# Turning the block inverses with 64x64 products through two shared banks, in a new order on TensorE

## The reference, cut to what matters

```python
DN_CHUNK = 64          # 16 value heads, computed in 8 pairs
def chunk_gated_delta(q, k, v, g, beta, s0):
    ...
    a = jnp.where(strict, jnp.einsum('bhncd,bhnsd->bhncs', kb, kc) * decay, 0.0)
    eye = jnp.eye(DN_CHUNK, dtype=F32)
    t_inv = lax.linalg.triangular_solve(eye + a, jnp.broadcast_to(eye, a.shape),
                                        left_side=True, lower=True, unit_diagonal=True)
    u = jnp.einsum('bhncs,bhnse->bhnce', t_inv, vb)
    w = jnp.einsum('bhncs,bhnsd->bhncd', t_inv, kb * jnp.exp(gc)[..., None])
    ...
def bidir_delta(q, k, v, g, beta, s0_f, s0_b):      # d = 0 forwards, d = 1 backwards
    ...
def rwkv7_scan(r, w, k, v, kk, a, reverse):         # second block, both directions
    def step(s, inp):
        sa = jnp.einsum('bhvk,bhk->bhv', s, -kk_t)
        s = (s * w_t[:, :, None, :] + sa[..., None] * (kk_t * a_t)[:, :, None, :]
             + v_t[..., None] * k_t[:, :, None, :])
```

## Time and profile before

| | |
|---|---|
| times of the kernel before, 3 runs | 2149.61, 2157.09, 2621.62 us; median 2157.09 |
| span of the profiled execution | 2156.7 us |
| the profiled execution beside the median | 0.4 us under it |
| TensorE busy | 1964.5 us (91%) |
| VectorE, ScalarE, GpSimd busy | 1031.2, 594.5, 74.1 us |
| level products of the first block, L1049 and L1076 | 60.5 and 58.1 us busy |
| copies of the turned inverses, L1195 | 47.8 us busy in 80 |

### The profile page before, as it was taken

The page is one execution under the profiler, slowest core; times in us unless marked ns, Lnnn a source line. Parts: engine busy times, 40 slices in busy tenths (PEclk is TensorE's granted clock), DMA queues, the critical chain, the costliest instruction groups (busy, mean ns, idle before and its releaser), DMA issues. The chain is left out here.

```text
span 2156.7 us, 40120 instructions
## 1 busy us (share of the span) xinstructions
PE 1964.5 (91%) x16700; PEld 1441.6 (67%) x16700; DVE 1031.2 (48%) x2064; ACT 594.5 (28%) x1275; POOL 74.1 (3%) x50
## 2 busy tenths in 40 slices
PE   5789999999999999789888889988889899989998
PEld 2346666666666666534376677767776798878887
DVE  3346756675766757411125457775455543311101
ACT  1023434444343434300203223232332321000000
POOL 0000101000010101000000000000000000000000
PEclk8889999999999999989999989989999999999999
DMA  8801101010101010032131243221112112434443
GB/s 329 313 18 61 38 24 60 2 60 1 61 1 61 1 61 1 2 117 78 39 122 40 78 169 118 105 106 46 36 56 91 71 65 80 175 117 156 156 176 137
DMA packets 52240, 184.73 MB, mean 86 GB/s; under 512 B 5856, under 2 KB 9312, under 8 KB 51552
## 3 DMA queue, kind: packets, MB, share of 16 engines
q1 hardware_dynamic: 52064, 182.23, 22.6%
HBM read 180.11 MB, written 2.10 MB: 84 GB/s over the span
## 5 line engine op out<-in xcount | busy, mean ns | idle before, releaser
L798 PE MATMUL banks<-u,w_ring 128*128 128x512 f32 x768 | 358.5, 603 | 6.4 <-PEq L195 6.4
L386 PE MATMUL banks<-u,w_ring 128*128 128x256 f32 x1056 | 251.9, 391 | 8.4 <-PEq L195 8.4
L798 PEld LDWEIGHTS banks<-u,w_ring 128*128 128x128 f32 x768 | 141.2, 193 | 134.3 <-issue 131.2
L386 PEld LDWEIGHTS banks<-u,w_ring 128*128 128x128 f32 x1056 | 200.4, 196 | 42.4 <-issue 17.1
L410 PE MATMUL banks<-u,w_ring 128*128 128x256 f32 x704 | 155.0, 384 | 4.8 <-PEq L195 4.8
L410 PEld LDWEIGHTS banks<-u,w_ring 128*128 128x128 f32 x704 | 135.7, 193 | 23.9 <-issue 5.0
L3239 PE MATMUL banks<-gated,w_ring 128*128 128x512 f32 (+1 forms) x384 | 140.7, 529 | 2.8 <-PEq L195 2.8
L3239 PEld LDWEIGHTS banks<-gated,w_ring 128*128 128x128 f32 x384 | 73.9, 193 | 69.2 <-issue 66.0
L826 DVE SCALAR_TENSOR_TENSOR acc<-raw,hc,acc 128x512 f32<-128x512 f32 x128 | 96.2, 752 | 4.6
L3239 PE MATMUL banks<-ffn,w_ring 128*128 128x256 f32 x352 | 77.9, 385 | 3.3 <-PEq L195 3.3
L3239 PEld LDWEIGHTS banks<-ffn,w_ring 128*128 128x128 f32 x352 | 68.0, 193 | 13.2 <-issue 3.7
(11 more groups left out here) (492 smaller groups left out, 3164.8 us busy)
## 6 DMA issues: line engine op xcount, KB each, us to landing
w_ring<-in_w SPq DMA_DIRECT2D x321, 512.0 KB, 6.2
h<-in_h SPq DMA_DIRECT2D x2, 2048.0 KB, 9.6
const_base<-in_const SPq DMA_DIRECT2D x1, 1216.0 KB, 5.5
hold<-h SPq DMA_DIRECT2D x1, 1024.0 KB, 6.2
const_part<-in_const SPq DMA_DIRECT2D x1, 1024.0 KB, 4.8
h<-hold SPq DMA_DIRECT2D x1, 1024.0 KB, 8.5
out<-u SPq DMA_DIRECT2D x8, 128.0 KB, 1.9
const_part<-in_const SPq DMA_DIRECT2D x1, 640.0 KB, 4.3
```

Of the source, the lines that this page charges most:

```text
L386: mm = self.nc.tensor.matmul(place, self.st.chunk(g % 2, slot)[:, P * k:P * k + P], self.src(k), start=(k == 0), stop=(k == KT - 1))
L798: mm = nc.tensor.matmul(self.places[m % len(self.places)][:, :], (st.slot(m) if g is None else st.chunk(g % 2, m))[:, P * k:P * k + P], u[ ...
```

## The change

Both blocks get the same edit. `turn` no longer uses 128x128 transposes: it multiplies each 64x64 block of `inv` by a 64x64 identity, 16 products (8 in the second block) of the same form as border and update. The blocks of partitions 0 to 63 go to bank 4 and those of 64 to 127 to bank 5, for either direction, so that both directions use the two banks in turn and a turn waits for the copy of the turn before it. The copy gathers from both banks. On TensorE update 0 moves ahead of turn 1, and turn 1 stands between the two updates. In the second block the keys' transposes and the own values, which stood ahead of update 0, now stand between turn 1 and update 1.

```diff
@@ -1052,13 +1052,13 @@
                 def turn(lv, d):
 
-                    if lv:
-                        pe.wait_ge(s["t_out"], due("t_out", 2 * (lv - 1) + d + 1))
+                    if lv or d:
+                        pe.wait_ge(s["t_out"], due("t_out", 2 * lv + d))
                     elif made:
                         pe.wait_ge(s["gate_in"], made.up("gate_in", 2))
-                    for t in range(TT):
-                        mm = nc.tensor.transpose(tile(bank[4 + d], t), inv[:, d, 2 * t:2 * t + 2, :].rearrange("p s e -> p (s e)"),
-                                                 C("ident"))
+                    for t, j, hb in quarters:
+                        mm = nc.tensor.matmul(bank[4 + hb][half(j), 64 * t:64 * t + 64], inv[half(hb), d, 2 * t + j, :], eye[half(hb), :],
+                                              start=True, stop=True)
                     mm.then_inc(s["t_turned"], 1)
@@ -1078,11 +1078,12 @@
                 for lv in range(1, LEVELS - 1):
-                    for d in range(2):
-                        border(lv, d)
-                        turn(lv - 1, d)
-                    for d in range(2):
-                        update(lv, d)
+                    border(lv, 0)
+                    turn(lv - 1, 0)
+                    border(lv, 1)
+                    update(lv, 0)
+                    turn(lv - 1, 1)
+                    update(lv, 1)
@@ -1192,7 +1193,9 @@
                             act.wait_ge(s["bc_done"], due("bc_done", 2 * (lv - 1) + d + 1))
-                        link(nc.scalar.activation(invt_c[:, d].rearrange("p s e -> p (s e)"), bank[4 + d][:, :], ACT.Copy), s["t_out"])
+                        link(nc.scalar.activation(invt_c[:, d].rearrange("p (t h) e -> p t h e", h=2),
+                                                  banks[:, 4:6, 0:2 * P].rearrange("p h (t e) -> p t h e", e=64), ACT.Copy),
+                             s["t_out"])
@@ -2224,19 +2227,20 @@
                 for lv in range(1, levels):
-                    for d in range(2):
-                        if lv == 1 and d == 1:
-                            pe.wait_ge(s["masked"], 1)
-                        border(lv, d)
-                        if lv == 1 and d == 0:
-                            pe.wait_ge(s["x_out"], 1)
-                        turn(lv - 1, d)
+                    border(lv, 0)
+                    if lv == 1:
+                        pe.wait_ge(s["x_out"], 1)
+                    turn(lv - 1, 0)
+                    if lv == 1:
+                        pe.wait_ge(s["masked"], 1)
+                    border(lv, 1)
+                    update(lv, 0)
+                    turn(lv - 1, 1)
                     if lv == 2 or lv == 3:
                         keys_turned(lv - 2)
                     if lv == 4:
                         own_values()
-                    for d in range(2):
-                        update(lv, d)
+                    update(lv, 1)
```

More of the change, by code:

```diff
@@ L2207, in turn @@
                 def turn(lv, d):
[L2209 to L2213, removed]
+                    if lv or d:
+                        pe.wait_ge(s["t_out"], 2 * lv + d)
+                    for t, hh, hf in quarters:
+                        mm = nc.tensor.matmul(bank[4 + hf][half(hh), at64(t)], inv[half(hf), d, 2 * t + hh, :], eye[half(hf), :],
+                                              start=True, stop=True)
                     mm.then_inc(s["t_turned"], 1)
@@ L2333, in _ @@
                             act.wait_ge(s["bc_done"], 2 * (lv - 1) + d + 1)
-                        link(nc.scalar.activation(inv_t[:, d, :, :].rearrange("p n e -> p (n e)"), bank[4 + d][:, 0:SEQ], ACT.Copy),
-                             s["t_out"])
+                        link(nc.scalar.activation(inv_t[:, d].rearrange("p (t f) e -> p t f e", f=2),
+                                                  banks[:, 4:6, 0:P].rearrange("p f (t e) -> p t f e", e=64), ACT.Copy), s["t_out"])
                     if lv == 1 or lv == 2:
```

## The result

The changed kernel takes **2232.35 us** (median of 4 runs, 2228.55 to 2234.88) against 2157.47 us before (4 runs beside it), a ratio of 1.036 with a 95% interval of 1.034 to 1.039: 75 us slower. The forecast was 2195, its range 2172 to 2228. The time lies in the rival "fetching is dearer" (2221 to 2235). The profiled execution has a span of 2232.7 us, 76 more than before. Two executions of the kernel before were far slower than all others (2621.62 us here, 10254.86 us beside the third group, with a granted clock of 0.178) and are in no ratio.

What follows compares the result with a forecast made beforehand. TensorE, busy 91% of the span, was taken to bound the kernel. First-block chain 28, instruction fetching 8 and second block 2.4 us sum to 38 over the 2157.1 us median: 2195 us, range 2172 to 2228.

Steps and rivals of the forecast that it cites:

- fetching is dearer: Rival, first block: each level 5.4 us, more holes and lower-clock stretches, 8 us a head, 64 in all; 2221–2235 us; chance 0.22.
- The copies on the path: First block: both ScalarE copies, hidden before, now delay the updates; 3.5 us a head, 28 us for eight.
- A level of 4.48 us: First block: three product sets of 0.46 us plus two rounds of 1.55, against 3.98 before.
- a round of 1.55: First block, turn start to the update using it: 0.82 to reader, 0.60 copy, 0.13 to update, in us.
- the 28: First block's chain cost in us: eight heads at 3.5, each 1.3 + 3 x 0.50 + 0.7.
- The instruction stream: First-block levels: loads rise from 136 to 192, 1.06 to 1.5 blocks at 3.6 us each; 8 us in all.
- I take 4.5 us for a head: First block: chain plus fetching per head, 1 us above the chain's 3.5, so 8 us more in all.
- its bound of 5: First block: upper bound of the fetch term per head, 3.6 us plus a second stretch at the lower clock.
- The second block: Chain cost there: 0.3 us in the last and in the first level, four pairs x 0.6 = 2.4 us.
- lie over the second copy, so I take nothing for them: Second block, levels 2 to 4: keys or values between turn 1 and update 1 hide the second copy; cost zero.
- At worst 0.3 a level: Second block, levels 2 to 4: worst case each pays the last level's 0.3 us; total bound plus 6 us.
- The holes: Fetch stalls in first-block levels; a rival at chance 0.10 had five of about 2.4 us go: 2183 or 2175 us.

Runs made afterwards that it cites:

- the third group: Kernels run side by side, all with late weight loads: 8 or 4 of 16 products per turn, or 128x128 transposes with adjacent turns; 2153.9, 2139.4, 2135.7 us.
- order_only: Kernel before with only the new TensorE order in the first block, keeping 128x128 transposes and separate banks per direction; 2189.6 us, ratio 1.018.
- late_own: Kernel before with first-block 64x64 turns in each direction's own banks, old order, and weight loads started after each head's levels; 2185.7 us, ratio 1.014.
- late_after: Changed kernel with each head's weight loads started only after its off-diagonal products; 2214.5 us, ratio 1.028 to before.
- late_own_8: late_own with only 8 of the 16 products in each turn and the copies scaled by zero, so output differs; 2153.9 us, ratio 0.999.
- second_only: Kernel before with the edit in the second block alone; 2165.5 us, ratio 1.005.

## Why the prediction was wrong

- **The copies on the path: right in the first block.** A level of 4.48 us was forecast and 4.5 measured where nothing else counts, a round of 1.55 against 1.53, level 1 plus 1.3 against 6.32 - 5.01 = 1.31 in six of eight heads. ScalarE's gathering copy takes 0.60 as the plain one did. The wait of update 1 was to be 0.9 us some 40 times; the wait of all updates for ScalarE is 41.6 us in 65 pieces, 0.39 and 0.85 in a level. order_only shows the path, not the 28: its 29.7 come from a longer chain (4.70 us a level, 36 us for eight heads without holes) less the holes that it lost.
- **The instruction stream: the mis-sized term.** "I take 4.5 us for a head", 8 us in all over the chain, should have been 63.8 - 28 = 36, if the 28 are taken as they stand. That is 4.5 on top of the 3.5 of the chain, for each head, where the forecast had 1, and just inside its bound of 5. The pace was not the error. 3.6 us a block was read from the earlier trace rows; head 5 of the changed kernel has it (3.6 as a mean), and late_own 3.76 and 3.89. The error was the use: the forecast set the fetch beside the chain, let the later of the two end decide, and worked that out for the one head with the longest hole, where the two came out nearly alike. From there to L1099 the changed kernel needs 26.7 us (392.7 to 419.4) for 737 loads, 5.8 blocks: 4.6 us a block. Two things are shown to be in that. Waits for copies and waits for instructions add: the first rise by 36 us and those ending in "issue" by 22, and in the changed kernel the next fetch starts 1.17 us after the end of a hole in the mean of the 19 holes behind which TensorE waits for no other engine, 2.18 in the mean of the other 17. A copy's wait there puts off the fetch itself, so the round of fetches is longer than 3.6. And a head at the lower clock in part (38 us of the levels against 17 before) is busy for 2.4 us longer (22.45 in head 2, 20.06 in head 5).
- **What remains of it.** 28 for the chain, 22 for issue waits and 6.5 for the clock (busy time over 8 x 20.06 is 13.9 us, over 8 x 20.65 it was 7.4) are 56 of the 64. The other 7 are not assigned. Fetches are 4.2 to 4.6 us apart in heads 0 to 3 and 3.6 to 3.8 in heads 4 to 7. The clock and the weights alone don't make that: late_after, in which no weights come in during the levels, still has some 4.2 in heads 0 to 2, at the full clock. A hole's place in the level moves from head to head, and with it whether a copy's wait falls behind it; that this makes the whole difference isn't shown.
- **The second block: too low.** Forecast 2.4 with bounds of minus 4 and plus 6, measured 9.7. The step that failed is "lie over the second copy, so I take nothing for them", which looked at TensorE alone. It left out the order on VectorE and ScalarE, where VectorE's work of L2374 (1.15 us) and the copies of x (1.21 us) now stand ahead of steps that the path waits for, in levels 2 and 5. "At worst 0.3 a level" had no row for these two, and the sum none for the clock, which here is at its lower level for 6.8 us more.
- **The holes.** They did not move away; in head 2 the hole closed 9.1 us after the start of level 1, before 9.5, as forecast. But it opened after 259 loads and not "after the same 179 loads": 80 more loads were through by then, since the turns of the two heads before it had brought 560 more, which is 80 short of five blocks of 128, and so shifted where a block ends. So fewer loads were left than the forecast had (737, not 817), and they still took 5 us longer (26.7, not 21.7). With the weight loads moved the holes of before go, and it gains 18 us.
- The rival that came true, "fetching is dearer", was worked out as each level at 5.4 and 8 us for a head, 64 in all; 63.8 were measured. So close a match is luck in part: the heads differ from 4.9 to 11.3 us, and levels 3 and 4 take 5.4 and 5.07 in head 5 but 5.96 in the mean of all.

## What to carry to other kernels

Count instructions as a resource of their own: where small products follow one another, 128 recorded loads with their matmuls want 3.7 to 3.9 us of fetching whatever they do, so four large transposes with dear changes of shape can be worth more than sixteen small ones without. Before an order is changed to share a bank, read the round from producer over copy to user, and on every engine what else is queued ahead of its steps; a copy that was hidden costs its whole round. And bulk loads that start beside a stretch rich in instructions hold those up: starting them behind it gave 18 us here, more than any order did.

## What was not expected of the hardware

- The pace of the instructions: 3.76 and 3.89 us for 128 loads with their matmuls, with DMA 2% busy.
- The round behind that pace: after a hole no fetch started until TensorE had gone on for at least 1.0 us, and a TensorE that waited for a block went on 2.2 to 2.9 us after its fetch had started. A wait for a copy in between comes on top.
- A bulk load puts off the start of a fetch: in head 2 of the kernel before the weights begin to come in at 361.05 and the next fetch starts at 368.06, 2.3 us before the hole closes; in head 2 of the changed kernel 383.75 and 390.35. The waits that end in "issue" fall from 12.5 to 2.3 us when the weights come in elsewhere.
- TensorE loses its clock at times, and the idle time alone doesn't tell when: in the changed kernel 38 us of the first block's levels are at the lower level (head 0 has a mean granted clock of 0.85, head 5 1.00 at nearly the same idle time), in late_after 20.5, and none in late_own_8, which waits 31 us in "issue". In the second block of second_only it fell with no hole, at 1493.59, behind a wait of 1.69 us for VectorE; the same wait in the third pair was not followed by a fall.
